# Mixer C of a two-layer encoder on one core: key thresholds by bitwise counting over pairs of tiles, keys turned between heads

## The reference, cut to what matters

```python
def indexer_scores(qi, wi, ki):
    s = jnp.einsum('bqhd,bsd->bqhs', qi, ki).astype(jnp.float32)
    return jnp.einsum('bqhs,bqh->bqs', jax.nn.relu(s), wi.astype(jnp.float32)) * (IDX_DIM ** -0.5 * IDX_HEADS ** -0.5)
...
            sc = indexer_scores(qiblk, wblk, ki)
            sc = jnp.where((key_chunk[None, :] <= q_chunk[:, None])[None], sc, -jnp.inf)
            _, idx = lax.top_k(sc, k_sel)
            valid = (idx // CHUNK) <= q_chunk[None, :, None]
            return selected_attention(qblk, gather_rows(k, idx), gather_rows(v, idx), valid)
```

## Time and profile before

| what | value |
|---|---|
| runs of the kernel before | 2778.16, 2786.86, 2780.9 us; median 2780.9 |
| the profiled execution, its own time | 2787.82 us |
| its span | 2786.1 us, 36346 instructions |
| TensorE, VectorE, ScalarE, GpSimd busy | 2648.5, 1546.6, 924.2, 194.3 us |
| mean granted TensorE clock | 0.953 of full |

### The profile page before, as it was taken

One profiled execution on the slowest core, in us unless ns is written; L12 is line 12 of the kernel. 1 busy time (PEld: TensorE's weight loads), 2 busy tenths in 40 slices (PEclk: granted clock), 3 DMA queues, 4 the chain that ended last, 5 costly groups with the idle time before them and its releaser, 6 DMA issues. The chain is left out here.

```text
span 2786.1 us, 36346 instructions
## 1 busy us (share of the span) xinstructions
PE 2648.5 (95%) x14198; PEld 2326.2 (83%) x14198; DVE 1546.6 (56%) x2791; ACT 924.2 (33%) x1762; POOL 194.3 (7%) x170
## 2 busy tenths in 40 slices
PE   7999999999999999989968988899999999999997
PEld 6778789989999998878757787797899898989896
DVE  2445363444444445566889899963734445354446
ACT  3207343322222232322044555462532232313232
POOL 0300040000000000310020000000400000000004
PEclk9999999999999999989965989889999999999999
DMA  4110311101010110131100000003211110101011
GB/s 138 44 42 1 113 49 48 61 30 60 30 60 30 44 46 31 68 102 31 44 8 1 1 1 1 1 13 131 67 43 34 39 52 30 60 30 60 30 46 65
DMA packets 81279, 124.25 MB, mean 45 GB/s; under 512 B 6224, under 2 KB 54736, under 8 KB 81168
## 3 DMA queue, kind: packets, MB, share of 16 engines
q1 hardware_dynamic: 81168, 122.74, 13.3%
HBM read 110.98 MB, written 11.75 MB: 44 GB/s over the span
## 5 line engine op out<-in xcount | busy, mean ns | idle before, releaser
L1132 DVE TENSOR_TENSOR act<-psum,act 128x512 f32<-128x512 f32 x540 | 367.6, 689 | 256.0 <-PE psum L1255 253.1
L1217 PE MATMUL psum<-xt_hi,layer_w_hi 128*128 128x384 f32 (+1 forms) x1536 | 506.1, 330 | 3.2 <-DVE xt_lo L847 3.2
L1219 PE MATMUL psum<-xt_hi,layer_w_lo 128*128 128x384 f32 (+1 forms) x1536 | 505.8, 329 | 0.0
L1218 PE MATMUL psum<-xt_lo,layer_w_hi 128*128 128x384 f32 (+1 forms) x1536 | 505.6, 329 | 0.0
L1253 PE MATMUL psum<-layer_w_hi,layer_h_split 128*128 128x512 f32 x1024 | 400.0, 391 | 2.8 <-DVE layer_h_split L1120 1.6
L1254 PE MATMUL psum<-layer_w_lo,layer_h_split 128*128 128x512 f32 x1024 | 399.4, 390 | 0.0
L1255 PE MATMUL psum<-layer_w_hi,layer_h_split 128*128 128x512 f32 x1024 | 399.1, 390 | 0.0
L1120 DVE TENSOR_TENSOR layer_h_split<-layer_h_raw,layer_h_split 128x384 fp32r<-128x384 f32 (+1 forms) x192 | 98.3, 512 | 351.5 <-ACT layer_h_split L1033 351.5
L1217 PEld LDWEIGHTS psum<-xt_hi,layer_w_hi 128*128 128x128 f32 x1536 | 289.0, 188 | 4.7 <-DVE xt_lo L847 3.5
L1218 PEld LDWEIGHTS psum<-xt_lo,layer_w_hi 128*128 128x128 f32 x1536 | 288.9, 188 | 1.3
L1219 PEld LDWEIGHTS psum<-xt_hi,layer_w_lo 128*128 128x128 f32 x1536 | 289.0, 188 | 0.0
(11 more groups left out here) (215 smaller groups left out, 4155.3 us busy)
## 6 DMA issues: line engine op xcount, KB each, us to landing
layer_w_raw<-in_ff_w SPq DMA_DIRECT2D x64, 1024.0 KB, 6.2
ab_in_w_raw<-in_ab_w_in SPq DMA_DIRECT2D x12, 512.0 KB, 4.2
c_in_w_raw<-in_c_w_in SPq DMA_DIRECT2D x12, 512.0 KB, 3.6
ab_in_xt_raw<-in_xT SPq DMA_DIRECT2D x8, 512.0 KB, 3.9
layer_resid<-in_x SPq DMA_DIRECT2D x16, 256.0 KB, 2.6
x_scratch<-act SPq DMA_DIRECT2D x8, 512.0 KB, 2.6
layer_resid<-x_scratch SPq DMA_DIRECT2D x16, 256.0 KB, 2.6
out_y_prompt<-act SPq DMA_DIRECT2D x8, 512.0 KB, 2.6
```

What stands on the lines that cost most here:

```text
L1132: dve.tensor_tensor(acc, banks[4 + g % 4][0:r], acc, ALU.add).then_inc(y_read, 1)
L1217: pe.matmul(out, w1_hi[:, k, w], xt_hi[:, k, a:b], start=(k == 0), stop=False)
L1218: pe.matmul(out, w1_hi[:, k, w], xt_lo[:, k, a:b], start=False, stop=False)
L1219: mm = pe.matmul(out, w1_lo[:, k, w], xt_hi[:, k, a:b], start=False, stop=(k == KT - 1))
```

## The change

- For tiles 7 to 3 the 256th largest score is found by bisection over the bits of the threshold. A counting round (`round_of_pair`) compares a tile's scores with a threshold per row, with the sum accumulated by the same instruction, for the two tiles of a pair (7 and 6, 5 and 4, 3 alone), then sets or drops one bit for both in two small steps. There are 32 rounds for each pair; the first finds the sign, and multiplies the scores by it in place.
- Tile 2 (384 keys) is ranked from below: 16 rounds of eight on the negated scores, in a copy. SAMPLE keeps its rounds of eight.
- A closing has five parts: turn the sign back, count the keys above the threshold and mark the equal ones, number the equal ones with a scan, make mask and admitted ties, add both. The parts stand at different heads.
- Rounds move: 14 of the first pair in `block_c_in`, 18 in heads 0 to 42; the second pair in heads 48 to 74, the third in 80 to 106, tile 2 in 112 to 124.
- In the set-up only the first key slot and the first queries are turned. The other ten slots are turned at heads 1, 4, ..., 28, each by the same instructions, on the two banks that probabilities and queries share.
- The turned indexer keys of `block_c_in` stay in place and are not made again. Indexer queries and products move to fixed heads (products of m = 3 to 6 from heads 30, 37, 66, 84). Score buffers become five and two that reuse parts of the first.
- The mask value becomes a power of two, and the scratch that the compiler keeps for GpSimd's DMAs becomes smaller.

```diff
+RING = 3
+SAMPLE_ROUNDS = TOPK_SAMPLE // 8
+BITS = 31
+PAIRED = [(1, 2), (3, 4), (5,)]
+FEW = 6
+FEW_ROUNDS = (nkeys(C_RANKED[FEW]) - TOPK) // 8
...
+    def round_of_pair(self, dve, k):
...
+        for n, m in enumerate(PAIRED[k]):
+            self.after(dve, m, k - 3)
...
+                ins = dve.tensor_scalar(ones, x, self.row_of(m, self.THRESHOLD), self.row_of(m, self.SHORT),
+                                        ALU.is_ge, ALU.add, accum_out=self.row_of(m, self.EXCESS))
+            self.step(m, ins)
+        self.after(dve, *PAIRED[k])
...
+            bit = 1 << (BITS - done)
+            dropped, threshold = every(self.DROPPED).bitcast(I32), every(self.THRESHOLD).bitcast(I32)
+            self.step(k - 3, dve.tensor_scalar(dropped, every(self.EXCESS).bitcast(I32), 31, bit,
+                                               ALU.arith_shift_right, ALU.bitwise_and))
+            self.after(dve, k - 3)
+            self.step(k - 3, dve.scalar_tensor_tensor(out=threshold, in0=dropped, scalar=bit >> 1, in1=threshold,
+                                                      op0=ALU.bitwise_xor, op1=ALU.bitwise_xor))
...
+        if part == 1:
+            self.step("spare", dve.tensor_scalar(nth, x, threshold, None, ALU.is_gt, ALU.add, accum_out=above))
+            self.step("spare", dve.tensor_scalar(equal, x, threshold, -MASKED, ALU.is_equal, ALU.mult))
+        if part == 2:
+            self.step("spare", dve.tensor_scalar(ties, above, float(TOPK), MASKED, ALU.subtract, ALU.mult))
+            self.step("spare", dve.tensor_tensor_scan(nth, equal, equal, 0.0, ALU.add, ALU.bypass))
+        if part == 3:
+            self.step(m, dve.tensor_scalar(x, x, threshold, MASKED, ALU.is_le, ALU.mult))
+            self.step("spare", dve.scalar_tensor_tensor(out=nth, in0=nth, scalar=ties, in1=equal, op0=ALU.is_le, op1=ALU.mult))
+        if part == 4:
+            self.step(m, dve.tensor_tensor(x, x, nth, ALU.add))
...
-                            ranking.take(dve, [0, 1] if x < rounds(0) - 8 else [1])
+                            ranking.round_of_pair(dve, 0)
+                            if x < SAMPLE_ROUNDS - 8:
+                                ranking.round_of_eight(dve, 0, ranking.scored(0))
...
+    KEY_ORDER = [0, 1, NP_TILES, NP_TILES + 1, OWN, *range(2, NP_TILES)]
+    KEY_AT = {1 + 3 * n: n + 1 for n in range(NS - 1)}
+    IDX_QUERY_AT = {24: 3, 29: 4, 60: 5, 76: 6}
+    ITEM_BASE = {3: 30, 4: 37, 5: 66, 6: 84}
...
+    spread(pairs_at, [0] * (BITS + 1 - 2 * ROUND_TILES), 0, 43)
+    spread(closes_at, [(1, part) for part in range(5)], 43, 48)
+    spread(pairs_at, [1] * (BITS + 1), 48, 75)
+    spread(closes_at, [(2, part) for part in range(5)], 49, 64)
+    spread(closes_at, [(3, part) for part in range(5)], 75, 80)
+    spread(closes_at, [(4, part) for part in range(5)], 81, 96)
+    spread(pairs_at, [2] * (BITS + 1), 80, 107)
+    spread(closes_at, [(5, part) for part in range(5)], 107, 112)
+    spread(few_at, ["open"] + ["round"] * FEW_ROUNDS + ["close"], 112, 125)
+    spread(closes_at, [(6, part) for part in range(5)], 125, 128)
...
-            for _ in range(ROUNDS_AHEAD):
-                ranking.take(dve, [1, 2])
...
-            for sl in range(NS):
-                r = srows(sl)
-                for part, (split, made) in enumerate(((kh, kh_made), (kl, kl_made))):
...
+            def keys(k):
+                sl = KEY_ORDER[k]
+                r = srows(sl)
+                for split, made in ((kh, kh_made), (kl, kl_made)):
+                    pe.wait_ge(made, k + 1)
+                    group([(kv * P, flat(split[0:r, k % 2, kv]), r) for kv in range(C_KV)], ident_r)
+                key_groups[sl] = n[0]
...
+                    if x in KEY_AT:
+                        keys(KEY_AT[x])
```

More of the change, by code:

```diff
@@ L28 @@
 F32R = mybir.dt.float32r
+I32 = mybir.dt.int32
+U8 = mybir.dt.uint8
 P = 128
@@ L1361, in relu, with step, after @@
                        scale=(HD * IDX_HEADS) ** -0.5).then_inc(self.relu_done, 1)
-    def step(self, m, ins):
+    def step(self, what, ins):
         self.steps += 1
-        self.last[m] = self.steps
+        self.last[what] = self.steps
         ins.then_inc(self.chain, 1)
+    def after(self, dve, *whats):
+        steps = max(self.last.get(what, 0) for what in whats)
+        if steps:
+            dve.wait_ge(self.chain, steps)
     def mix(self, dve, m, i):
@@ L1400, in take, with rows_of, row_of @@
-    def take(self, dve, ranks):
-        self.find(dve, ranks)
-        self.mark(dve, ranks)
-    def close(self, dve, m):
-        dve.wait_ge(self.chain, self.last[m])
-        self.step(m, dve.tensor_scalar(self.scored(m), self.scored(m), TAKEN, MASKED, ALU.not_equal, ALU.mult))
+    def rows_of(self, k, what):
+        return self.ranked.state[:, k % 2, what, 0:len(PAIRED[k])]
+    def row_of(self, m, what):
+        k, n = (0, 0) if m == FEW else pair_of(m)
+        return self.ranked.state[:, k % 2, what, n:n + 1]
@@ new lines, in eight, with round_of_eight, close_sample, few @@
+    def eight(self, m):
+        return self.ranked.top8[0:rows(C_RANKED[m])]
+    def round_of_eight(self, dve, m, x):
+        self.after(dve, m)
+        self.step(m, dve.max(self.eight(m), x))
+        self.after(dve, m)
+        self.step(m, dve.match_replace(x, self.eight(m), x, TAKEN))
+    def close_sample(self, dve):
+        x = self.scored(0)
+        self.after(dve, 0)
+        self.step(0, dve.tensor_scalar(x, x, TAKEN, MASKED, ALU.not_equal, ALU.mult))
+    def few(self):
+        return self.spare[:, 0, 0:nkeys(C_RANKED[FEW])]
@@ new lines, in open_few, with close_few, close @@
+    def open_few(self, dve):
+        self.after(dve, FEW, 5, "spare")
+        self.step(FEW, dve.tensor_scalar(self.few(), self.scored(FEW), -1.0, None, ALU.mult))
+    def close_few(self, dve):
+        self.after(dve, FEW)
+        self.step(FEW, dve.max(self.eight(FEW), self.few()))
+        self.after(dve, FEW, 2 - 3)
+        self.step(FEW, dve.tensor_scalar(self.row_of(FEW, self.THRESHOLD), self.eight(FEW)[:, 0:1], -1.0, None, ALU.mult))
+    def close(self, dve, m, part):
+        x = self.scored(m)
+        nk = x.shape[1]
+        k = 0 if m == FEW else pair_of(m)[0]
+        equal, nth = [self.spare[:, n, 0:nk] for n in range(2)]
+        threshold, above, ties = [self.row_of(m, what) for what in (self.THRESHOLD, self.EXCESS, self.TIES)]
+        self.after(dve, m, "spare", k - 3)
+        if part == 0 and m != FEW:
+            sign = self.row_of(m, self.SIGN)
+            self.step(m, dve.tensor_scalar(threshold, threshold, sign, None, ALU.mult))
+            self.step(m, dve.tensor_scalar(x, x, sign, None, ALU.mult))
+        if part == 1:
[9 more added lines that the diff above has]
+            self.step(m, dve.tensor_tensor(x, x, nth, ALU.add))
+            self.last["spare"] = self.steps
@@ L2032, in scores @@
                 if h == 0:
-                    pe.wait_ge(copied, query_groups[p])
+                    pe.wait_ge(copied, max([query_groups[p]] + [key_groups[slot0(t) + b] for b in range(blocks(t))]))
                 out = banks_of(("head", x))
@@ L2064, in values @@
                 mm.then_inc(o_done, 1)
-            for sl in range(NS):
-                r = srows(sl)
-                for part, (split, made) in enumerate(((kh, kh_made), (kl, kl_made))):
-                    pe.wait_ge(made, sl + 1)
-                    if sl >= 2:
-                        pe.wait_ge(k_copied, 2 * (sl - 2) + part + 1)
-                    for kv in range(C_KV):
-                        mm = turn(banks[2 * part + sl % 2], kv * P, flat(split[0:r, sl % KRING, kv]))
-                    mm.then_inc(k_turned, 1)
+            keys(0)
             for g in range(4):
```

289 lines of the change are left out of this document (144 added, 145 removed).

## The result

The changed kernel takes 2760.8 us (median of 5 runs, 2757.2 to 2767.1) against 2785.6 for the kernel before beside it (5 runs, 2778.2 to 2791.2): a ratio of 0.9921 with a 95% interval of 0.9901 to 0.994. It is faster by about 25 us (0.8%), a third of the 74 forecast, and its time is above the range's upper end of 2750. The profiled execution took 2760.0 us, against 2714 that the sum gives on the profiled scale: 46 us are missing.

The account below looks back on a forecast made before the run. It costed stages one by one, bound by VectorE or TensorE: nine tile stages at 384 us against 435.2 (51 off) plus 22.8 from set-up, 74 off the 2780.9 median, giving 2707 us; range 2680 to 2750.

Parts of the forecast that it names:

- The set-up's saving: Mixer C's set-up: first score near 1415.7 instead of 1438.5, saving 22.8 us.
- Rivals one and two: VectorE counts: one, half a pass, 2687 us (0.09); two, over one pass, 2789 us (0.06) or slower still (0.06).
- The direction: Whole kernel: faster by more than 0.3%, chance 0.88.
- p0, p1 and p7: First, second and eighth of mixer C's nine tile stages, p0 to p8: forecast at 29.5, 40 and 36 us.
- TensorE covers it, so it costs nothing: Input stage: dearer counting rounds add 7.4 us of VectorE, hidden behind TensorE; without that cover, 7.4 us.
- I take p2 at full clock: Third tile stage: indexer products raise the clock, TensorE needs 26 us, under VectorE's 32.7; stage 37 us.
- The count: VectorE counting rounds: one pass plus 0.08 us a count; a round of tiles 5 and 4 costs 2.17 us.
- The scan: VectorE closings: a scan takes one pass; at half throughput four scans would add an estimated 3.1 us.
- a stage takes about a tenth more than the busier: Tile stages where two engines are close: length about a tenth over the busier engine's time.
- GpSimd has room: Mixer's tile stages: GpSimd, busy 2.4 us a stage, can take the keys' subtractions between heads.
- Rival three: Mixer heads stall: exposed key slots, clock 0.50 through p2, shared banks, uneven heads; 2743 us (2728 to 2765), chance 0.19.

Follow-up runs that it names:

- e1: Changed kernel with three of the input stage's 14 counting rounds moved into the mixer's first 43 heads: 2757.8 us, ratio 0.9916.
- c1: Changed kernel with e9, e11, GpSimd's subtractions in pieces, and five and eight input-stage rounds for seven and seven: 2722.0 us, ratio 0.9782.
- e6: Changed kernel with two unread ballast products of 512 columns added to each head of p1 and p2: 2765.9 us, ratio 0.9951.
- e10: Changed kernel with four unread ballast products of 512 columns in each of heads 41 to 47: 2766.5 us, ratio 0.9932.
- c2: c1 with the indexer products of tiles 3 and 4 moved from heads 30 to 42 to heads 21 to 34: 2719.1 us, ratio 0.9773.
- e12: Changed kernel whose later counts take one operand by row and a constant zero, so thresholds are not found: 2756.8 us, ratio 0.991.
- e11: Changed kernel with one counting round a head, second pair from head 43, third from 75: 2742.8 us, ratio 0.9854.
- e9: Changed kernel with ScalarE's next exp ahead of query and key copies and TensorE's value products ahead of their turns: 2747.3 us, ratio 0.987.
- e2: Changed kernel with GpSimd's low-part subtractions for keys and queries cut to one head each, altering score precision: 2746.6 us, ratio 0.9872.
- e4: Changed kernel with all eleven key slots turned in the set-up again, none between heads: 2786.1 us, ratio 1.002.

## Why the prediction was wrong

**Right.** The set-up's saving (22.8 forecast, 22.3 measured). Rivals one and two: a count is neither half a pass nor two. The direction. p0, p1 and p7 came within 2.1 us, p0 and p1 by luck: p1's 40 was TensorE's 39.8 at a clock of 0.50, and TensorE was busy 31.8 us at 0.72 of it; in p0 TensorE's 26.7 came out at 24.5, and VectorE, at 26.1 for 23.1, was the busier.

**The input stage: the step "TensorE covers it, so it costs nothing".** It cost 6.6 us, near the 7.4 that the prediction named as the price without the cover. The busy share (143.93 of 147) hid that TensorE's next weights hang on VectorE: what waits behind the rounds in VectorE's queue was not asked. e1 shows the chain and its end, and in c1, too, the mixer starts at 1407.3.

**The clock: the step "I take p2 at full clock".** p2 had a clock of 0.57, as before, and TensorE's 40.64 us there became 46.22, about what four products of 1.42 us more cost at half clock. The step had taken 23.2 + 2.8 for TensorE instead, so that VectorE's 32.7 set the stage. The prediction read from the earlier trace rows that indexer products bring the clock up. In p2 of the changed kernel the clock was full from 1495.2 to 1502.0, before the first of the six products (1495.68), and behind that it stayed at 0.50 over four of them (1505.8 to 1524.3) to the end of the stage:

```profile
1502.00:1532.20 30.20, 28.58 (x132) 19.47 (x131) 22.05 (x53) 13.98 (x47) 2.38 (x1) 0.50 0.00 1
```

In the kernel before, the rise behind the first products, at 1542.6, was soon followed by p3 (1548.8), whose clock is full throughout; which of the two kept it up there wasn't tried. e6, e10 and c2 show that neither ballast nor another place of the products makes p1 and p2 cheaper. That p2 can be had at 37 us was not shown, and why its clock stays low is open.

**The count: a term mis-sized.** 0.12 us on each count, for two operands by row (e12): a round of tiles 5 and 4 took 2.37 us (1570.25 to 1572.62), not 2.17. In p3 that is 19 x 0.20 = 3.8 us. With the step that GpSimd held (2.2 us) it is 6.0, of which VectorE's busy time shows 2.9 over the forecast (72.72 for 69.8): other terms of the stage were a little dear.

**The scan: the value chosen.** Two passes (2272 ns), the value that the prediction cites from the Trainium skill ("DVE: opcode table, instruction layouts, handler registers and perf-mode slots", section "Datapath and trigger behaviour": half throughput) and not the one it took: 1.05 us over a pass for 1024 columns, so 3.0 for the 2944 of the four scans named.

**The coupling: the step "a stage takes about a tenth more than the busier".** Two mechanisms stand in its place. Two rounds in one head cost more than one round in each of two: with the rounds spread evenly p4 took 5.0 us less with as much VectorE work, and the clock fell no more in p3 to p6 (e11). And two waits on ScalarE came out in the query heads, most clearly in p6 (e9); that VectorE hid them before is read, not tried. A third price, GpSimd holding VectorE's small steps, was in no sum: "GpSimd has room" counted only its own time (7.5 us of the stages; e2).

**Rival three** comes nearest in time, 2728 to 2765, and it had 0.19. Where it spoke, its numbers were close: p0 to p2 at 120.7 us for 124, p3 to p5 at 199.3 for 199. Its uneven heads and its shared banks were right. Its key slots were not (6.4 us for ten, not 1.9 each; e4), and the clock was not at 0.50 all through p2 but at 0.72 in p1 and 0.57 in p2, so that its p0 to p2 came out by luck in part. These effects overlap and don't add: e1 won nothing alone, and c1 more than the upper end of what was expected of its parts.
